# The last dense layer's down product with tokens as rows of the array's output, in a three-block fp32 network on one core

## The reference

```
def rmsnorm(x, g):
    xf = x.astype(jnp.float32)
    y = xf * lax.rsqrt(jnp.mean(xf * xf, axis=-1, keepdims=True) + EPS)
    return (y * g.astype(jnp.float32)).astype(x.dtype)
...
        hf = rmsnorm(x, norm_ffn_g[l])
        gate, up = jnp.split(hf @ w_ffn_in[l], 2, axis=-1)
        x = x + (jax.nn.silu(gate) * up) @ w_ffn_out[l]
    return rmsnorm(x, final_norm_g)
```

## Time and profile before

| | us |
|---|---|
| median of three runs | 2007.54 (2007.24 to 2014.68) |
| profiled execution, its own time | 2004.65 |
| profiled execution, span | 2002.8 |
| TensorE busy | 1962.8 |
| VectorE busy | 1529.3 |
| ScalarE busy | 1214.5 |

### The profile page before, as it was taken

One profiled execution on the slowest core, in us unless ns is written; L12 is line 12 of the kernel. 1 busy time (PEld: TensorE's weight loads), 2 busy tenths in 40 slices (PEclk: granted clock), 3 DMA queues, 4 the chain that ended last, 5 costly groups with the idle time before them and its releaser, 6 DMA issues.

```text
span 2002.8 us, 32075 instructions
## 1 busy us (share of the span) xinstructions
PE 1962.8 (98%) x12418; PEld 1736.1 (87%) x12418; DVE 1529.3 (76%) x1656; ACT 1214.5 (61%) x1297; POOL 64.2 (3%) x105
## 2 busy tenths in 40 slices
PE   8999999999999999999999999999999999999997
PEld 7799998688888888888888888889988889999997
DVE  7776554889998999899989988996486568776662
ACT  4264443777777777777877778774354555545442
POOL 3020000000000000000000000001000100030000
PEclk8999999999999999999999999999999999999999
DMA  6635453499999999999999999984532434454551
GB/s 253 176 127 183 175 191 125 149 363 373 355 372 363 365 373 356 372 366 366 371 357 373 359 371 364 363 330 149 197 108 96 148 107 151 165 185 174 189 189 43
DMA packets 75865, 510.26 MB, mean 255 GB/s; under 512 B 8320, under 2 KB 14464, under 8 KB 14592
## 3 DMA queue, kind: packets, MB, share of 16 engines
q1 hardware_dynamic: 75776, 508.98, 68.2%
HBM read 506.66 MB, written 2.29 MB: 254 GB/s over the span
## 4 chain that ended last, share of the span: by engine, by line
PE 88%; DVE 5%; ACT 2%; issue 2%; DMA 2%; POOL 1%; SPq 0%; ACTq 0%; DVEq 0%; POOLq 0%
PE ps L924 9%; PE ps L928 9%; PE ps L656 9%; PE ps L927 9%; PE ps L659 9%; PE ps L660 9%; PE ps L949 5%; PE ps L953 5%; PE ps L952 5%; PE ps L1224 2%; PE ps L1226 2%; PE ps L1227 2%; PE ps L1150 1%; PE ps L935 1%; PE ps L685 1%
## 5 line engine op out<-in xcount | busy, mean ns | idle before, releaser
L1973 DVE TENSOR_TENSOR ring_r<-ring,high 128x2048 fp32r<-128x2048 f32 x227 | 517.4, 2289 | 53.6 <-ACT high L1612 31.8
L1612 ACT ACTIVATE high<-ring 128x2048 fp32r<-128x2048 f32 x224 | 428.7, 1914 | 14.1 <-DMA ring<-w_stream 13.0
L1846 DVE TENSOR_TENSOR ring_r<-ring,high 128x2048 fp32r<-128x2048 f32 x126 | 288.8, 2296 | 118.9 <-ACT high L1415 118.5
L927 PE MATMUL ps<-ring_r,big_r 128*128 128x512 f32 x896 | 349.0, 390 | 0.0
L659 PE MATMUL ps<-scr_r,high 128*128 128x256 f32 (+1 forms) x1200 | 343.3, 286 | 0.0
L1415 ACT ACTIVATE high<-ring 128x2048 fp32r<-128x2048 f32 x126 | 239.5, 1907 | 163.6 <-PE ps L656 89.2
L1973 DVE TENSOR_TENSOR ring_r<-ring,scr_r 128x2048 fp32r<-128x2048 f32 x112 | 256.3, 2288 | 39.3 <-ACT scr_r L1612 39.0
L656 PE MATMUL ps<-sq_r,high 128*128 128x272 f32 (+1 forms) x832 | 239.0, 287 | 5.0 <-DVE scr_r L1864 5.0
L660 PE MATMUL ps<-sq_r,ring_r 128*128 128x272 f32 (+1 forms) x832 | 238.5, 287 | 0.0
L659 PEld LDWEIGHTS ps<-scr_r,high 128*128 128x128 f32 x1200 | 227.9, 190 | 0.2
L1612 ACT ACTIVATE scr_r<-ring 128x2048 fp32r<-128x2048 f32 x112 | 214.5, 1915 | 16.8 <-DMA ring<-w_stream 16.8
(11 more groups left out here) (503 smaller groups left out, 3922.9 us busy)
## 6 DMA issues: line engine op xcount, KB each, us to landing
ring<-w_stream SPq DMA_DIRECT2D x477, 1024.0 KB, 4.8
big<-spread SPq DMA_DIRECT2D x32, 146.0 KB, 3.0
spread<-big SPq DMA_DIRECT2D x8, 151.0 KB, 5.0
h<-h_in SPq DMA_DIRECT2D x1, 1088.0 KB, 5.1
out<-hn SPq DMA_DIRECT2D x1, 1024.0 KB, 4.7
vec<-vec_in SPq DMA_DIRECT2D x1, 576.0 KB, 8.2
```

The costliest lines, as they stand in the source:

```text
L927: pe.matmul(o, x_item_high[:, k, :], w_low[:, cols], start=False, stop=False)
L1612: act.activation(w_high, w, ACT.Copy).then_inc(S["moe_high"], 1)
L1846: dve.tensor_tensor(w_low, blocks_at(c, 0, CH), w_high.bitcast(F32), ALU.subtract).then_inc(S["weights_low"], 1)
L1973: dve.tensor_tensor(w_low, w, w_high.bitcast(F32), ALU.subtract).then_inc(S["moe_low"], 1)
```

## The change

The down part of the last dense layer is turned: now the hidden values (128 channels x 128 tokens) stand in the array and the weights move, 512 columns at a time. The output has tokens on the partitions: two token tiles t, each with two halves of 512 channels, in four PSUM banks (6, 7 for t = 0 and 4, 5 for t = 1) that stay open over all 22 steps of k. `x` is added in PSUM by matmuls with the identity as the moving operand, in plain fp32. The host lays the down weights out k by k, four blocks of 256 columns each, so that a chunk holds two k. The last two k are done bank after bank, so that the banks end one after the other. The squares are summed along the row by ScalarE's accumulator; root and reciprocal have one value per token; the gain, a row of 1024 values, is copied to all partitions by the host and fetched by its own DMA (512 KB) once the weight loads are issued. Four output DMAs of 256 KB write tokens x channels. Two semaphores are merged into one (`wo_done`) to make room. The first block's dense layer is as before, only split into `ffn_in` and `ffn_out`.

```diff
+        out_gain = h_old[:, 0:D]
+        out_gained = h_old[:, D:2 * D].rearrange("p (t c) -> p t c", t=2)
+        out_squares = sq[:, :, :].rearrange("p k t -> p (k t)")[:, 0:2 * D].rearrange("p (n c) -> p n c", n=4)
+        out_tok = hn_old[:, 0:2 * D].rearrange("p (t c) -> p t c", t=2)
+        def out_bank(t, half):
+            return (6, 4)[t] + half
+        def out_step(t, n):
+            return S["normed"], 8 * len(PLAIN_NORMS) + 4 * t + n + 1
...
SyncE
-            sp.wait_ge(S["normed"], normed_at(10, 7))
-            sp.dma_start(out, hn256).then_inc(S["out_done"], 16)
-            sp.wait_ge(S["out_done"], 16)
+            sp.wait_ge(S["wo_done"], 2 * KD)
+            sp.dma_start(out_gain, gain_in).then_inc(S["vec_landed"], 16)
+            for t in range(2):
+                sp.wait_ge(S["out_scaled"], t + 1)
+                sp.dma_start(out[t][:, 0:512], out_tok[:, t, 0:512]).then_inc(S["out_done"], 16)
+                sp.wait_ge(*out_step(t, 3))
+                sp.dma_start(out[t][:, 512:], out_tok[:, t, 512:]).then_inc(S["out_done"], 16)
+            sp.wait_ge(S["out_done"], 64)
...
TensorE
+            def out_products(k, w_high, w_low, t, half, first=False):
+                rows, cols = slice(t * P, (t + 1) * P), slice(512 * half, 512 * (half + 1))
+                o = ps[:, out_bank(t, half), :]
+                begun(first, pe.matmul(o, hid_high[:, k, rows], w_high[:, cols], start=False, stop=False))
+                pe.matmul(o, hid_high[:, k, rows], w_low[:, cols], start=False, stop=False)
+                return pe.matmul(o, hid_low[:, k, rows], w_high[:, cols], start=False, stop=(k == KF - 1))
+            def out_by_token(b_out):
+                for t in range(2):
+                    for half in range(2):
+                        claim(out_bank(t, half))
+                    for k in range(KD):
+                        pe.matmul(ps[:, out_bank(t, k // 4), k % 4 * P:(k % 4 + 1) * P], x[:, k, t * P:(t + 1) * P],
+                                  ident[:, :], start=(k % 4 == 0), stop=False)
+                for k in range(KF - 2):
+                    pe.wait_ge(S["ffn_hid"], KF + k + 1)
+                    _, _, first = parts_of(b_out + 4 * k)
+                    c, at = (b_out + 4 * k) // CH, (b_out + 4 * k) % CH
+                    w_high, w_low = parts_at(c, at, at + 4)
+                    for t in range(2):
+                        for half in range(2):
+                            out_products(k, w_high, w_low, t, half, first and t == 0 and half == 0)
+                pe.wait_ge(S["ffn_hid"], 2 * KF)
+                b = b_out + 4 * (KF - 2)
+                assert b % CH == 0
+                _, _, first = parts_of(b)
+                for t in range(2):
+                    for half in range(2):
+                        for n in range(2):
+                            w_high, w_low = parts_at(b // CH, 4 * n, 4 * n + 4)
+                            mm = out_products(KF - 2 + n, w_high, w_low, t, half, first and t == 0 and half == 0 and n == 0)
+                        mm.then_inc(S["ffn_down"], 1)
...
-            ffn(1, 9, "ffn3", SEQ, in_low, hid_high, hid_low, BOFF["ffn3_in"], BOFF["ffn3_out"],
-                lambda j, k: None, lambda j: sum_tiles(10, SEQ, range(4)) if j == 2 else None)
-            sum_tiles(10, SEQ, range(4, KD))
+            ffn_in(1, 9, "ffn3", SEQ, in_low, BOFF["ffn3_in"])
+            out_by_token(BOFF["ffn3_out"])
...
ScalarE
-            norm(10, x, SEQ, lambda k: act.wait_ge(S["ffn_out"], 8 + k + 1))
+            act.activation(warm, eps_col, ACT.Sqrt)
+            for t in range(2):
+                for half in range(2):
+                    act.wait_ge(S["ffn_down"], KD + 2 * t + half + 1)
+                    if half == 0:
+                        act.wait_ge(*out_step(t, 0))
+                    squared = act.activation(out_squares[:, 2 * t + half, :], ps[:, out_bank(t, half), :], ACT.Square, scale=1.0 / 32,
+                                             accum_out=out_sum[:, t, half:half + 1])
+                    if half == 0:
+                        squared.then_inc(S["sq_ready"], 1)
+                    else:
+                        step(squared)
+                act.wait_ge(*out_step(t, 1))
+                act.activation(out_std[:, t, 0:1], out_sum[:, t, 1:2], ACT.Sqrt, bias=out_eps[:, t, 0:1])\
+                   .then_inc(S["std_ready"], 1)
+                act.wait_ge(*out_step(t, 2))
+                act.activation(out_tok[:, t, 0:512], out_gained[:, t, :], ACT.Copy, scale=out_root[:, t, 0:1])\
+                   .then_inc(S["out_scaled"], 1)
...
VectorE
-                for m in range(KD):
+                for m in range(KD) if n == 0 else ():
...
-            norm(10, x, hn, "final3_g", SEQ)
+            split_weights(NCH - 1)
+            dve.wait_ge(S["vec_landed"], 32)
+            for t in range(2):
+                dve.wait_ge(S["ffn_down"], KD + 2 * t + 1)
+                dve.tensor_tensor(out_gained[:, t, :], ps[:, out_bank(t, 0), :], out_gain[:, 0:512], ALU.mult)\
+                   .then_inc(S["normed"], 1)
+                dve.wait_ge(S["sq_ready"], 8 * 10 + t + 1)
+                dve.tensor_scalar(out_eps[:, t, 0:1], out_sum[:, t, 0:1], EPS, None, ALU.add).then_inc(S["normed"], 1)
+                dve.wait_ge(S["std_ready"], 10 + t + 1)
+                dve.reciprocal(out_root[:, t, 0:1], out_std[:, t, 0:1]).then_inc(S["normed"], 1)
+                dve.wait_ge(*out_step(t, 2))
+                dve.scalar_tensor_tensor(out=out_tok[:, t, 512:], in0=ps[:, out_bank(t, 1), :], scalar=out_root[:, t, 0:1],
+                                         in1=out_gain[:, 512:], op0=ALU.mult, op1=ALU.mult).then_inc(S["normed"], 1)
...
host
-    parts.append(blocks(a["w_ffn_out_3"][0]))
+    parts.append(a["w_ffn_out_3"][0].reshape(KF, P, 4, WIDE).transpose(0, 2, 1, 3).reshape(-1, P, WIDE))
```

More of the change, by code:

```diff
@@ L55 @@
     ("pool_scale", 8), ("mix_g0", 8), ("mix_g1", 8), ("ffn_g0", 8), ("ffn_g1", 8), ("final_g", 8),
-    ("pre_g", 8), ("post_g", 8), ("mix3_g", 8), ("ffn3_g", 8), ("final3_g", 8),
+    ("pre_g", 8), ("post_g", 8), ("mix3_g", 8), ("ffn3_g", 8),
     ("conv3", 6 * 4), ("lru_ba", 2), ("lru_bx", 2), ("lru_lam", 2), ("ig_b", 1), ("fg_b", 1),
@@ L123 @@
         HBEFORE[_c] = _part[_n - HIGH] if _n >= HIGH else None
-PLAIN_NORMS = [0, 1, 3, 4, 5, 7, 10]
+PLAIN_NORMS = [0, 1, 3, 4, 5, 7]
 SUMMED = [2, 3, 4, 5, 6, 9]
@@ L204, in moba_slope, with program @@
     return float(np.float32(2.0 ** (-8.0 * (2 * h + 2) / 16)))
-def program(nc, w_stream, vec_in, h_in, out):
+def program(nc, w_stream, vec_in, h_in, gain_in, out):
     with ExitStack() as ctx:
@@ L386, in program @@
         merged_high3 = h_old_r[:, 0:KD * SEQ].rearrange("p (k t) -> p k t", k=KD)
+        out_gain = h_old[:, 0:D]
+        out_gained = h_old[:, D:2 * D].rearrange("p (t c) -> p t c", t=2)
+        out_squares = sq[:, :, :].rearrange("p k t -> p (k t)")[:, 0:2 * D].rearrange("p (n c) -> p n c", n=4)
+        out_tok = hn_old[:, 0:2 * D].rearrange("p (t c) -> p t c", t=2)
+        out_sum, out_eps, out_std, out_root = (small[:, 208 + 4 * n:212 + 4 * n].rearrange("p (t c) -> p t c", t=2)
+                                               for n in range(4))
         part3 = scr[:, 3072:3072 + 1536].rearrange("p (b n k) -> p b n k", b=2, n=3)
@@ L404, in program @@
                     cmp_kv_ready score_done s_ready exp_ready prob_ready turn_done turned pv_done y_ready
-                    br_done br_part br_ready wo2_done wo2_ready
+                    br_done br_part br_ready wo_done wo2_ready
                     in3_done in3_act in3_dve if_done conv3_ready qk_silu lru_g_done lru_sig lam_exp
@@ L410, in program @@
                     sb_z_done sb_zs sb_ln sb_lk sb_r_done sb_arg sb_a sb_o_done sb_y
-                    out3_done out3_part merged wo3_done x3_ready out_done""".split():
+                    out3_done out3_part merged x3_ready out_scaled out_done""".split():
             S[n] = sem(n)
@@ L763, in _, with ffn_in @@
                 bank_owner[b + 1] = (S["x_ready"], 2 * j + 2)
-            def ffn(n, norm_i, split_n, t, x_low, hidden_high, hidden_low, b_in, b_out, inside, behind):
+            def ffn_in(n, norm_i, split_n, t, x_low, b_in):
                 for p in range(KF):
@@ L773, in ffn, with ffn_out @@
                         sum_squares(norm_i, t)
-                if n == 0:
-                    pe.wait_ge(S["normed"], normed_at(3, KD - 1))
+            def ffn_out(n, t, hidden_high, hidden_low, b_out, inside, behind):
+                pe.wait_ge(S["normed"], normed_at(3, KD - 1))
                 for j in range(4):
@@ L815, in pool_behind @@
                     pool_products(j - 1)
-            ffn(0, 2, "ffn0", T0, in_low_ffn0, hid_high0, hid_low0, BOFF["ffn0_in"], BOFF["ffn0_out"],
-                pool_inside, pool_behind)
+            ffn_in(0, 2, "ffn0", T0, in_low_ffn0, BOFF["ffn0_in"])
```

(18 more changed lines are left out.)

## The result

The changed kernel takes 2016.5 us (median of 10 runs, 2014.11 to 2019.24) against 2007.9 for the kernel before (10 runs, same chip): a ratio of 1.0040, 95% interval 1.0029 to 1.0050. That is 8.6 us slower where 7.5 us faster was predicted, outside the range. The profiled execution took 2017.14 us with a span of 2015.4; for the kernel before these were 2004.65 and 2002.8.

What follows compares the result with a forecast made beforehand. TensorE's product stream and the serial tail were taken as the bound; -3.4 (products) - 1.7 (sums of squares) + 3.5 (residual) - 5.9 (tail) = -7.5 us on the 2007.54 median gave 2000.0 us, range 1996.0 to 2004.0.

Steps and rivals of the forecast that it cites:

- What bounds the kernel now: Whole kernel: TensorE's stream sets the down part, then a 12.4 us serial tail; only these two stretches change.
- Wide products: Down part: 264 products of 512 columns at 0.2271 us replace 528 narrow ones, 59.95 us, gain 3.4 us.
- two narrow products save only 2.5 ns: Down part, by the skill's lone-gap formula: 264 x 0.0025 = 0.7 us saved, making the sum 2.7 us worse.
- Residual: Head of the down part: 16 plain fp32 identity products run as 32 instructions, adding 3.5 us on the path.
- rival 2: Cheaper residual (-1.7), wide products (-3.6) or tail (-1.2), two of them together: about -11, 1996.5 us; chance 0.16.
- rival 3: Head of the down part: the residual's loads and products don't overlap, 14.9 instead of 3.5 us, 2011.4; chance 0.03.
- Chunks and the gain: Down part: shorter weight chunks and the gain's DMA, issued some 30 us ahead of use, cost nothing.
- The tail: Kernel's end, after the last product: rebuilt chain takes 6.5 us against 12.4, gain 5.9 us.
- T: The end of the last product, from which the forecast counts the times of the kernel's end; span's end at T+6.5.
- the queueing that I had put at about 1 us: Kernel's end: tile 1's first multiplication and square wait behind tile 0's scalings, pushing tile 1 about 1 us behind TensorE.
- Rival 1: Output at the end: a quarter DMA keeps the whole's 5.06 us, +2.1, 2002.1 us; chance 0.12.

Runs made afterwards that it cites:

- e1: The changed kernel with eight unused columns behind the vectors' tile, so later SBUF tiles stand where they stood before: 1999.32 us against 2006.47, ratio 0.9965.
- e8: The realigned changed kernel without the 16 identity products that add x: 1996.56 us against 2007.55 for the kernel before, ratio 0.9943.
- g2: The kernel before with only big, scr and the rest moved 32 bytes, h to sq where they were: 2017.86 us, ratio 1.0057.
- g1: The kernel before with h, x, hn, sq moved 32 bytes and big, scr and the rest 256 bytes: 2014.76 us, ratio 1.0038.
- e4: The kernel before with every tile moved 32 bytes, distances kept: 2007.58 us against 2006.47, ratio 1.0009.
- f4: The kernel before with all tiles moved by 128 bytes, distances kept; its measured time is not in the text given.

## Why the prediction was wrong

**The step that failed** is one sentence in "What bounds the kernel now": "The change touches these two stretches only; the other 1925 us stay." They became 1944.45. I read the diff for instructions and did not price the line that took a column out of a table, since it changes no instruction in the experts' stage. It changed their addresses. The miss is 2016.5 - 2000.0 = 16.5 us. By medians, putting the addresses back moves the kernel from 8.6 slower to 7.15 faster: 15.7 us of the 16.5, and what is left is within the scatter of the medians. Where I had put nothing for the 1925 us, the experts' stage lost 17 us in the trace. None of my rivals was about a stage that the diff leaves alone.

**The rest of the steps** can be checked in e1, which is the change without that accident. Its 7.15 us by median stand against the predicted 7.5, and 1999.3 against 2000.0. Term by term:

```profile
1925.56 3.73 PE L820 MATMUL ps<-ident,x 128*128 128x128 f32 x32
1929.05 0.48 PE L810 MATMUL ps<-high,big_r 128*128 128x512 f32 x1
...
1988.76 0.39 PE L812 MATMUL ps<-high,big_r 128*128 128x512 f32 x1
```

- *Wide products.* From 1929.05 to one pace behind the last start, 1988.76 + 0.23 = 1988.99, are 59.94 us for 264: 0.2270 each. Predicted 59.95 from the earlier trace rows. Only the first three distances are a run-in: 316, 233 and 231 ns. (The prediction's "two narrow products save only 2.5 ns" has the sides swapped; its 0.7 us is right.) In the kernel as changed the same stretch is 1947.94 to 2009.62, 61.68 us, 0.2336 each: 1.7 us of the accident lie here.
- *Residual.* 1925.56 to 1929.05, 3.49 us; predicted 3.5 from the earlier trace rows. e8 says the same from the other side. The single passes of rival 2 (1.8) and rival 3 (14.9) are out.
- *Chunks and the gain.* TensorE is busy for all 63.44 us of the window above. ScalarE and VectorE keep about 43 and 39 us of slack. In the kernel as changed the gain is issued at 1977.14, 28.6 us ahead of its use at 2005.69, near the predicted 30, and lands 5.5 us later. That is more than the 4.7 I had quoted for twice the bytes, but far from late.
- *The tail.* The last product starts at 1988.76 and T is about 1989.15. The chain of e1 from there, and its last issues (start us, us, what):

```profile
1987.79 0.75 DVE hn L2615
1988.54 0.61 DVE h L2608
1989.23 0.93 ACT sq L1872 x3
1990.29 0.21 ACT sq L1872
1990.53 0.30 ACT small L1879
1990.86 0.17 DVE small L2613
1991.06 0.75 DVE hn L2615
```

```profile
1991.80 0.33 SPq L617 DMA_DIRECT2D out<-hn  x1
...
1992.18 0.43 SPq L619 DMA_DIRECT2D out<-hn  x1
```

```profile
out<-hn SPq DMA_DIRECT2D x4, 256.0 KB, 2.2
```

The multiplication of tile 1's first bank starts at 1988.54, right behind tile 0's scaling (1987.79 + 0.75), though the bank was ready 0.75 earlier: the queueing that I had put at about 1 us. The two squares take 1.26 us (1989.23 to 1990.49) where I had twice 0.79: the second starts while the first one's accumulator is still being read. The second scaling ends at 1991.81, T+2.7 where T+3.0 was predicted. The last DMA is issued at T+3.0 instead of T+3.5. It needs 2.7 us from there to the end of the span, predicted 2.9; the 2.2 in the row above are to the landing, which for the old DMA was 4.7 of its 5.06. The span ends at 1994.9, T+5.8, predicted T+6.5. So 0.3 of these 0.7 us are the scaling, 0.1 to 0.2 the issue, 0.2 the DMA, and 0.1 my rounding up. Rival 1, that a quarter keeps the whole's 5.06, is out.

The trace of e1 from the down part's start is 69.34 us (1925.56 to 1994.9) against 77.65: 8.3 faster, against 7.5 predicted, and the difference is this tail. So the kernel's own part was priced to within 1 us and the result missed by 16, on something that needed 0 instructions.

**What was there to see.** The kernel before kept its tiles at multiples of 512 bytes from one another. Nothing in its profile shows what leaving that costs, for no wide product in it is off that grid. It does show that the pace of 227 ns is not a constant of the instruction: the run-in behind each unit's transpositions has 231 to 236. But the question "which addresses does this diff move" could be answered from the declarations alone: `vec` stands in the middle of the allocations, and 32 bytes move 4032 wide products of the experts' stage. At 1 ns each that is 4 us, over half of the gain at stake; measured, it was over 4 ns each. A rival with that price would have been worth a tenth of the chances, and a wider range on the slow side.

## What to carry to other kernels

List what a diff moves in SBUF as well as what it executes. A removed constant, a scratch tile or a resized table shifts every later tile, and a 2 to 3% slower matmul over thousands of instructions shows no wait anywhere: look for it by laying start-to-start distances of one group side by side, in their order, not in the busy shares. When a change loses before the first instruction it touches, put the addresses back with a few unused columns (e1: 8.6 us slower became 7.15 faster, the fastest complete version here) before judging the change itself.

## What the hardware showed that I had not expected

- Products of 512 moving fp32r columns over a 128x128 standing tile settle at one start in 227 ns when the two operands' SBUF starts lie 0, 256 or 512 bytes off the old distances (all multiples of 512), and about every 232 to 234 ns (single distances 226 to 241, mostly 230 to 236) at 32 to 128 bytes off. Cost in this kernel: 11.8 us (64 bytes) to 19.4 us (96 bytes). Products of 256 and 272 columns stay at 120 to 121 ns in the mean.
- The pace of such a stream has a memory. Behind an interruption, or behind products at an off distance, it takes some seven products to come back to 227 ns (before, g2), and more than eleven in g1; at an off distance it goes round in a short cycle and does not come back (234, 231, 235, 233 in the turned part of the changed kernel).
- The mechanism is not shown. It is not the absolute address (e4, f4), nor a wait, the clock (1.00), traffic (DMA share 0.01 in the window above) or what the other engines touch (idle in the same window). A collision of the next tile's load with the moving read would fit, since that load runs beside the product before it; no run isolates it. Also open is what sets the length of the cycle and the exact pace at each distance. Of the distances between 128 and 256 only the change's own, 32 bytes down, was measured (232.8 ns in the mean over its trace).
- The Trainium skill ("SBUF — State Buffer", Operand start alignment) speaks of which operand starts are legal; all those here are, and the runs show that legal starts still differ by 2 to 3% in a wide product.
